# One-hot rows of the routing made by subtract, abs and relu in place of a compare

## What is computed

```
s = einsum('nhpd,hpkd->nhpk', q, sub_keys)          # 8 heads, 2 halves, 128 keys each
sv, si = lax.top_k(s, 16)                            # the best 16 of each half
cand = sv[:, :, 0, :, None] + sv[:, :, 1, None, :]
fv, fi = lax.top_k(cand, 16)                         # the best 16 pairs
eidx = take_along_axis(si0 * 128 + si1, fi)
g = softmax(fv)
act = gelu(einsum('nhkd,nd->nhk', expert_u[eidx], x))
out = einsum('nhk,nhkd->nd', g * act, expert_v[eidx])
```

## Time and profile before

| what | value |
|---|---|
| median of 3 runs | 1991.54 us (1986.9 to 1997.16) |
| the profiled execution | 1984.43 us, span 1982.7 us |
| PE, PEld busy | 95%, 91% of the span |
| DVE, ACT, POOL busy | 69%, 44%, 46% |
| `search`, 654 to 1389 us | 37% of the span |
| L1663 (the compares) | POOL x360, 329.3 us; DVE x56, 12.8 us |

### The profile page before, as it was taken

How to read it: one execution, slowest core, us unless ns; L and a number is a source line. 1 busy time by engine, 2 the same in 40 slices (tenths; PEclk the granted TensorE clock), 3 DMA queues, 4 the chain that set the end, 5 groups by cost and what they waited for, 6 DMA issues and landing times. The chain is left out here.

```text
span 1982.7 us, 32456 instructions
## 1 busy us (share of the span) xinstructions
PE 1889.2 (95%) x11529; PEld 1799.5 (91%) x11529; DVE 1365.5 (69%) x2638; ACT 880.2 (44%) x1917; POOL 915.5 (46%) x790
## 2 busy tenths in 40 slices
PE   6999999998889999999999899999999999999998
PEld 6988778887889998898898899999999999999997
DVE  3136746665432799798989777777678787777775
ACT  4021123334332337587778688883333333333333
POOL 4425322421324359699999887772122222222210
PEclk9999999998999999999999899999999999999999
DMA  7632189987621345998999899999799999999982
GB/s 175 114 98 78 56 219 280 279 253 248 149 63 24 116 136 188 275 277 268 285 275 278 257 304 320 325 309 334 254 344 329 352 339 336 352 332 343 351 302 92
DMA packets 325956, 481.10 MB, mean 243 GB/s; under 512 B 37628, under 2 KB 250108, under 8 KB 322468
## 3 DMA queue, kind: packets, MB, share of 16 engines
q1 hardware_dynamic: 287724, 341.63, 56.1%
q0 software_dynamic: 36864, 134.23, 21.1%
q10 hardware_dynamic: 1208, 3.16, 0.5%
HBM read 393.81 MB, written 83.97 MB: 241 GB/s over the span
## 5 line engine op out<-in xcount | busy, mean ns | idle before, releaser
L1473 PE MATMUL ps<-x_high,split_high 128*128 128x416 f32 x1024 | 371.4, 363 | 8.4 <-DVE split_low L1460 5.0
L1473 PE MATMUL ps<-x_high,split_low 128*128 128x416 f32 x1024 | 362.2, 354 | 0.0
L1473 PE MATMUL ps<-x_low,split_high 128*128 128x416 f32 x1024 | 360.4, 352 | 0.0
L2103 PE MATMUL ps<-hid_high,split_high 128*128 128x416 f32 x1024 | 358.9, 350 | 1.5 <-PEq L1686 1.5
L2103 PE MATMUL ps<-hid_low,split_high 128*128 128x416 f32 x1024 | 358.8, 350 | 0.0
L2103 PE MATMUL ps<-hid_high,split_low 128*128 128x416 f32 x1024 | 358.7, 350 | 0.0
L1663 POOL TENSOR_SCALAR area<-iota_row,chosen 128x128 f32<-128x128 f32 x360 | 329.3, 927 | 2.5
L1342 POOL DMA_INDIRECT gathered_rows<-in_peer_v_dram,gathered_index x128 | 135.3, 1057 | 417.0 <-DVE gathered_acc L1379 351.0
L2046 ACT CAST split_high<-area 128x1024 fp32r<-128x1024 f32 x127 | 133.3, 1049 | 383.4 <-PE ps L2103 382.6
L2074 DVE TENSOR_TENSOR split_low<-area,split_high 128x1024 fp32r<-128x1024 f32 x127 | 155.6, 1225 | 134.3 <-ACT split_high L2046 134.3
L1473 PEld LDWEIGHTS ps<-x_high,split_high 128*128 128x128 f32 x1024 | 193.7, 189 | 14.9 <-DVE split_low L1460 8.1
(11 more groups left out here) (289 smaller groups left out, 3803.5 us busy)
## 6 DMA issues: line engine op xcount, KB each, us to landing
area<-in_peer_v_dram SPq DMA_DIRECT2D x128, 512.0 KB, 5.5
u_nat<-in_peer_u_dram SPq DMA_DIRECT2D x392, 128.0 KB, 5.8
routing<-dense SPq DMA_DIRECT2D x26, 1024.0 KB, 6.4
area<-hidden SPq DMA_DIRECT2D x128, 208.0 KB, 7.4
hidden<-gelu_out SPq DMA_DIRECT2D x124, 208.0 KB, 4.4
w_raw<-in_w_in_dram SPq DMA_DIRECT2D x44, 512.0 KB, 5.9
mv_nat<-in_peer_u_dram SPq DMA_DIRECT2D x120, 128.0 KB, 3.7
u_nat<-turned_u SPq DMA_DIRECT2D x30, 512.0 KB, 3.8
```

Source lines behind the costliest of these rows:

```text
L1473: ins = self.nc.tensor.matmul(self.k.ps[:, b, 0:N], w[:, b, kk, :], x[:, kk, 0:N], start=(kk == 0 and p == 0), stop=(kk == KD - 1 and p == 2))
L2103: ins = nc.tensor.matmul(ps[:, kk, 0:N], v[:, b, kk * P:(kk + 1) * P], h[:, b, :], start=(n == 0 and p == 0), stop=(n == P - 1 and p == 2))
```

## The change

GpSimd no longer compares. It subtracts: for `apart` it adds the negated second index to the row of column numbers, 4 times 128x128 per batch, and for `first` (where DVE doesn't make it) it subtracts the first index, 4 times again, all one step earlier than the batch's step. ScalarE then takes the absolute value of four frames in one instruction of 128x512, for `apart` and for `first`, and turns `first` into a one-hot by relu(1 - |d|) in one more. VectorE's 14 batches are made by one `is_equal` of 128x512 with both operands spread by broadcast. To have a semaphore left for `subtracted`, two early loads share one: `vc_loaded` is now `wg_loaded`, and PE waits for 32 in place of 16.

```diff
-    vc_loaded, wg_loaded, line_stored, stored = sem("vc_loaded"), sem("wg_loaded"), sem("line_stored"), k.stored
+    wg_loaded, line_stored, stored = sem("wg_then_vc_loaded"), sem("line_stored"), k.stored
+    vc_loaded = wg_loaded
...
-                    pe.wait_ge(vc_loaded, 16)
+                    pe.wait_ge(vc_loaded, 32)
...
-    def first_rows(eng, b, ready):
-
-        eng.wait_ge(pick_out, turns(plan.turned_for(b)))
-        after(eng, routed, b - AREAS + 1)
+    def both_by(b):
+
+        return b + 1 + sum(i not in plan.on_vector for i in range(b + 1))
+
+    def subtract(pool, b):
+
+        pool.wait_ge(pick_out, turns(plan.turned_for(b)))
+        after(pool, second_ready, b - 1)
         for f in range(FEW):
             c = plan.column(b) + f
-            ins = eng.tensor_scalar(first[:, b % AREAS, f, :], iota[:, :], chosen[:, 0, c:c + 1], None, ALU.is_equal)
-        ins.then_inc(ready, 1)
+            ins = nc.gpsimd.tensor_scalar(apart[:, b % 2, f, :], iota[:, :], chosen[:, 1, c:c + 1], None, ALU.add)
+        ins.then_inc(subtracted, 1)
+        if b not in plan.on_vector:
+            after(pool, routed, b - AREAS + 1)
+            for f in range(FEW):
+                c = plan.column(b) + f
+                ins = nc.gpsimd.tensor_scalar(first[:, b % AREAS, f, :], iota[:, :], chosen[:, 0, c:c + 1], None, ALU.subtract)
+            ins.then_inc(subtracted, 1)
+
+    def first_rows(dve, b):
+
+        c = plan.column(b)
+        dve.wait_ge(pick_out, turns(plan.turned_for(b)))
+        after(dve, routed, b - AREAS + 1)
+        nc.vector.tensor_tensor(first[:, b % AREAS], bcast(iota[:, :], 1, FEW), bcast(chosen[:, 0, c:c + FEW], 2, P), ALU.is_equal
+                                ).then_inc(vector_first_ready, 1)
...
-                for b in plan.routing.get(n, []):
-                    if b not in plan.on_vector:
-                        first_rows(pool, b, first_ready)
+                for b in plan.routing.get(n + 1, []):
+                    subtract(pool, b)
...
                 for b in plan.routing.get(n, []):
-                    act.wait_ge(pick_out, turns(plan.turned_for(b)))
-                    after(act, second_ready, b - 1)
-                    for f in range(FEW):
-                        c = plan.column(b) + f
-                        ins = nc.scalar.activation(apart[:, b % 2, f, :], iota[:, :], ACT.Abs, bias=chosen[:, 1, c:c + 1])
-                    ins.then_inc(apart_done, 1)
+                    act.wait_ge(subtracted, both_by(b))
+                    nc.scalar.activation(apart[:, b % 2], apart[:, b % 2], ACT.Abs).then_inc(apart_done, 1)
+                    if b not in plan.on_vector:
+                        nc.scalar.activation(first[:, b % AREAS], first[:, b % AREAS], ACT.Abs).then_inc(apart_done, 1)
...
                 for b in plan.routing.get(n, []):
-                    act.wait_ge(apart_done, b + 1)
+                    act.wait_ge(apart_done, both_by(b))
+                    if b not in plan.on_vector:
+                        nc.scalar.activation(first[:, b % AREAS], first[:, b % AREAS], ACT.Relu, bias=1.0, scale=-1.0).then_inc(first_ready, 1)
                     after(act, routed, b - AREAS + 1)
```

More of the change, by code:

```diff
@@ L1654, in search @@
         "first_ready", "second_ready", "apart_done", "routed", "batch_out"))
-    vector_first_ready = sem("vector_first_ready")
-    def first_rows(eng, b, ready):
-        eng.wait_ge(pick_out, turns(plan.turned_for(b)))
-        after(eng, routed, b - AREAS + 1)
+    vector_first_ready, subtracted = sem("vector_first_ready"), sem("subtracted")
+    def both_by(b):
[3 more added lines that the diff above has]
+        after(pool, second_ready, b - 1)
         for f in range(FEW):
             c = plan.column(b) + f
-            ins = eng.tensor_scalar(first[:, b % AREAS, f, :], iota[:, :], chosen[:, 0, c:c + 1], None, ALU.is_equal)
-        ins.then_inc(ready, 1)
+            ins = nc.gpsimd.tensor_scalar(apart[:, b % 2, f, :], iota[:, :], chosen[:, 1, c:c + 1], None, ALU.add)
[12 more added lines that the diff above has]
+                                ).then_inc(vector_first_ready, 1)
     group_stored = [sem("group_stored0"), sem("group_stored1")]
@@ L1980, in step @@
                     if b in plan.on_vector:
-                        first_rows(dve, b, vector_first_ready)
+                        first_rows(dve, b)
                 for m in plan.dots.get(n, []):
```

## The result

The changed kernel takes 2241.18 us in the median (2240.64 to 2245.32, 4 runs) against 1992.89 of the kernel before beside it: a ratio of 1.125, 95% interval 1.122 to 1.128, 248 us slower. The profiled execution has a span of 2238.9 us against 1982.7.

The account below looks back on a forecast made before the run. POOL was taken to bound the first routing stretch, 850 to 1100 us. Terms -12 - 3 + 2 + 3 = -10 us, rounded to -11, took 1991.5 to 1980.5 us; the 8-in-10 range was 1958 to 2105.

Parts of the forecast that it names:

- R2: Rival: on POOL, all routing steps, subtraction costs like the compare, 0.59 us: +175 to +330, 2170 to 2320; chance 0.33 including middle.
- What bounds the kernel: POOL bounds the first routing stretch, 850 to 1100 us, with 25 to 35 us to give; the second has nothing.
- t, the time of one subtraction: One 128x128 pointer-operand subtraction on POOL takes 0.26 us, bounds 0.20 and 0.59; saves 12 us, plus 3 before 850 us.
- sum for the sort stretch, 5.66 us per step: POOL per step, 850 to 1100 us: 8.96 x 0.26 + 1.68 + 1.65 = 5.66 us against 5.97.
- The rule on loops that compare: On GpSimd, compare-and-select loops run at 2.03 cycles per element, 1.03 unrolled; so one subtraction takes below 0.30 us.
- R2's arithmetic: At 0.59 us per subtraction: first stretch 8.6 to 10.3 us per step, +100 to 168; second 6.9 to 8.4, +55 to 115.
- standing still: POOL's stalls while DVE works: 0.375 us per compare, counted per step as 1.68 us in the first stretch.
- The middle value of R2: Subtraction of 0.42 us on POOL: 7.1 to 8.2 us per first-stretch step, 5.7 to 6.4 second; 2035 to 2105; chance 0.14.
- ACT's work: ScalarE's four-frame instructions, 0.65 us each, fit: one-batch step 4.96 us, 0.5 to spare; costs 1 to 2 us, 20 uncovered.
- ACT's wait: ScalarE newly waits for POOL's subtractions, with copy, `second`, gelu and rounding behind; charged 3 us, bounds -5 and +15.
- DVE's batches: VectorE's 14 batches, one instruction each, save 3 to 6 us in the second stretch where nobody waits for DVE: 0.
- the shared semaphore: `wg_loaded` and `vc_loaded` lie far apart in SP's order; PE's wait for 32 needs both: 0.

Follow-up runs that it names:

- three kernels: Slower kernels with more GpSimd instructions: the changed kernel 2241.18 us, only `apart` subtracted by GpSimd 2210.78, the kernel before with four additions per compare group 2190.47.
- the last two kernels: Kernel before with only `first` subtracted by GpSimd, one batched instruction per batch: 1977.84 us, ratio 0.995; the same for every other GpSimd batch: 1976.79 us, 0.994.
- batched version of the changed kernel: Changed kernel with each four GpSimd subtractions in one broadcast `tensor_tensor` of 128x512: 2010.94 us, ratio 1.011.
- first experiment: Changed kernel with only `first` made the new way, `apart` back on ScalarE's four `Abs`: 2007.94 us, ratio 1.008.
- third experiment: Kernel before with four additions ahead of each of GpSimd's 90 groups of compares, two early loads sharing a semaphore: 2190.47 us, ratio 1.100.

## Why the prediction was wrong

The forecast was 1980.5 us and the chip gave 2241.2. The case that came true is R2, which had 0.33 and a price of 2170 to 2320; the stated range, up to 2105, left it out.

- *What bounds the kernel*: held. POOL was the bound of the sort stretch: adding to it costs at once (three kernels), and with it free and ScalarE heavier some 7 to 12 us are won (the last two kernels).
- *t, the time of one subtraction*: the step that failed. I took 0.26 us, "between the affine select and the cast"; it is 0.592 in the kernel and 0.607 alone, the end I had named "the nearest in form". I chose by the kind of work where the form of the instruction sets the time. The 128x128 compare's 590 was not read as a cost of its form because an affine select, another form, has 0.28. With 0.592 in place of 0.26 the prediction's own sum for the sort stretch, 5.66 us per step, becomes 8.6.
- *The rule on loops that compare*: by the Trainium skill's GPSIMD Engine Reference, Performance pitfalls for Q7 kernels, I took t to be below 0.30 us. That doesn't hold for this instruction, which measures 0.59 to 0.62 us for all four operations; the section speaks of loops in Q7 kernels.
- *R2's arithmetic*: held. In the sort stretch it gave 8.6 us per step if standing still is counted per step and 10.3 if per instruction; measured 9.14. Standing still was (634.8 - 776 x 0.592) / 98 = 1.8 us per step of the routing. By place it held too: by the gelus of steps 19, 78 and 117, the steps with sorts lost 152 us (R2 with what it adds before 850: 120 to 213) and those after them 96 (55 to 115), at 8.03 us per step (6.9 to 8.4).
- *The middle value of R2*: its upper ends were worked out too low. At t = 0.42, with standing still per instruction as at the upper end of R2, a step takes 8.96 x (0.42 + 0.375) + 1.65 = 8.8 us and not 8.2, and 7.1 and not 6.4 in the second stretch. That adds some 170 us and not 115, so the stated range should have gone to about 2160; the measured time lies beyond that too.
- *ACT's work*: the cover held. In the batched version of the changed kernel, whose ScalarE program is the same, ACT is busy 200 of 250 us in the sort stretch, and in the step shown above it works from 1028.50 on without a gap and ends the rounding 4.66 us later, against 4.96 foretold. The four-frame instructions are 0.61 to 0.63 us, as taken. Only the kernels that keep the four pointer `Abs` are fuller, with 231 and 245.
- *ACT's wait*: I put 3 us, and 2 for its work. In the changed kernel the wait for POOL is 349 us, but that is t's cost and not one of its own. With POOL's added time gone, 15 us (first experiment) and 22 us (batched version) are left for ScalarE's work, its wait and what GpSimd and VectorE do to each other; no run takes these apart.
- *DVE's batches and the shared semaphore*: 0 foretold; the former measured 0.1%, 3 us, by itself. The latter is part of the third experiment and wasn't tried by itself.

## What to carry to other kernels

Price an added instruction by the nearest row of the same form (opcode, pointer or immediate operand, shape), not by what it computes; where two readings lie a factor of two apart and the engine is full, ask what the change costs at the dearer one before choosing. Of an engine that is full in a stretch, count the instructions that a change leaves it: the trace may blame another engine, which only stands at the semaphore. To relieve GpSimd here, one broadcast two-input instruction per four frames saved more than half of the time, and a change of operation nothing. Look then at what its longer instructions do to VectorE.

## What was not expected of the hardware

A pointer `tensor_scalar` of 128x128 on GpSimd takes 0.607 us for each of the four operations tried, a two-input subtraction of the same size 0.455: the second tensor is cheaper than the scalar. Of 128x512, a two-input subtraction over plain operands takes 1.26 us and over broadcast ones 1.04. And 194 two-input instructions of 1.04 us on GpSimd, in place of 360 compares, raised the mean of VectorE's dot product from 1278 to 1608 ns; with 90 of them it is 1330, with 45 (and 180 compares) 1286.
